# The chunk scan of a Mamba-2 SSD encoder in another order, its skip term as a TensorE product

## The reference, cut to what matters

```python
seg = acs[:, :, :, None] - acs[:, :, None, :]
decay_in = exp(where(tri, seg, NEG_INF))
cb = einsum('bctgn,bcsgn->bctsg', cc, bc)
y_diag = einsum('bctsg,bctsgh,bcsghp->bctghp', cb, decay_in, xdt)
states = einsum('bcsgn,bcsgh,bcsghp->bcghpn', bc, decay_out, xdt)
# scan over chunks: h = h * chunk_decay + states, prev = h before the chunk
y_off = einsum('bctgn,bcghpn,bctgh->bctghp', cc, prev, exp(acs))
# forward and backward direction, then
y = y_fwd + y_bwd + d_skip * xs
y = y * silu(z)                      # then a grouped RMSNorm
# gMLP: mixed = w_s @ v (per 128-token chunk) + b_s;  out = gelu(u) * mixed
```

## Time and profile before

| | |
|---|---|
| time before, median of 3 runs | 2483.04 us (2482.91 to 2487.15) |
| the profiled execution's own time | 2485.22 us |
| its span in the profile | 2483.4 us |
| TensorE matmul busy | 2426.9 us (98%) |
| VectorE, ScalarE, GpSimd busy | 1375.8, 998.4, 1263.1 us |
| granted TensorE clock, mean | 0.996 |
| scan, first state product to first y_turn, layer 0 | 65.25 us |
| the same in layer 1 | 65.85 us |

### The profile page before, as it was taken

How to read it: one execution, slowest core, us unless ns; L and a number is a source line. 1 busy time by engine, 2 the same in 40 slices (tenths; PEclk the granted TensorE clock), 3 DMA queues, 4 the chain that set the end, 5 groups by cost and what they waited for, 6 DMA issues and landing times.

```text
span 2483.4 us, 33046 instructions
## 1 busy us (share of the span) xinstructions
PE 2426.9 (98%) x12882; PEld 2072.2 (83%) x12882; DVE 1375.8 (55%) x1561; ACT 998.4 (40%) x1737; POOL 1263.1 (51%) x814
## 2 busy tenths in 40 slices
PE   7999999999999999999999999998999999999999
PEld 6989997887888888887898899977878888888887
DVE  4476557738655546428345765586385555544332
ACT  4345567613444344212024465585144344431110
POOL 3242113323977877666633311142349877866664
PEclk9999999999999999999999999999999999999999
DMA  4434444231222212654333334442212222226544
GB/s 160 136 114 125 134 139 149 81 119 68 85 79 91 85 68 85 217 178 132 130 121 94 110 128 151 134 136 90 89 64 102 85 70 100 83 90 201 174 141 142
DMA packets 102964, 290.68 MB, mean 117 GB/s; under 512 B 7800, under 2 KB 30328, under 8 KB 101112
## 3 DMA queue, kind: packets, MB, share of 16 engines
q1 hardware_dynamic: 80360, 255.73, 30.4%
q10 hardware_dynamic: 22456, 32.90, 4.1%
HBM read 229.84 MB, written 58.75 MB: 116 GB/s over the span
## 4 chain that ended last, share of the span: by engine, by line
PE 81%; DVE 9%; ACT 4%; POOL 3%; issue 2%; DMA 1%; SPq 0%; ACTq 0%; DVEq 0%; POOLq 0%
PE PS L690 20%; PE PS L694 20%; PE PS L693 20%; PE PS L775 3%; PE PS L779 3%; PE PS L778 3%; PE PS L945 2%; PE PS L934 2%; POOL WL L629 2%; DVE HL L1780 1%; PE PS L1116 1%; PE PS L1081 1%; PE PS L924 1%; PE PS L923 1%; ACT LG L1501 1%
## 5 line engine op out<-in xcount | busy, mean ns | idle before, releaser
L605 POOL CAST WH<-RAW 128x1024 fp32r<-128x1024 f32 x156 | 184.5, 1182 | 905.5 <-PE PS L690 327.1
L690 PE MATMUL PS<-HH,WH 128*128 128x512 f32 x1264 | 496.4, 393 | 3.6 <-ACT QS L1668 2.6
L694 PE MATMUL PS<-HH,WL 128*128 128x512 f32 x1264 | 493.3, 390 | 0.0
L693 PE MATMUL PS<-HL,WH 128*128 128x512 f32 x1104 | 430.5, 390 | 0.0
L607 POOL TENSOR_TENSOR WL<-RAW,WH 128x1024 fp32r<-128x1024 f32 x156 | 396.8, 2543 | 12.5
L690 PEld LDWEIGHTS PS<-HH,WH 128*128 128x128 f32 x1264 | 237.4, 188 | 56.5 <-DVE HL L1780 3.5
L694 PEld LDWEIGHTS PS<-HH,WL 128*128 128x128 f32 x1264 | 237.3, 188 | 51.9
L690 PE MATMUL PS<-AR,WH 128*128 128x512 f32 x704 | 276.0, 392 | 2.3 <-DVE X L2208 1.8
L694 PE MATMUL PS<-AR,WL 128*128 128x512 f32 x704 | 275.9, 392 | 0.0
L693 PE MATMUL PS<-AR,WH 128*128 128x512 f32 x704 | 275.2, 391 | 0.0
L775 PE MATMUL PS<-WH,HH 128*128 128x256 f32 (+1 forms) x896 | 261.0, 291 | 1.7 <-ACT KN L1307 1.3
(11 more groups left out here) (274 smaller groups left out, 4677.3 us busy)
## 6 DMA issues: line engine op xcount, KB each, us to landing
RAW<-wst SPq DMA_DIRECT2D x156, 512.0 KB, 3.5
TOE<-toe_d SPq DMA_DIRECT2D x64, 512.0 KB, 3.7
act_d<-CVV SPq DMA_DIRECT2D x22, 1024.0 KB, 4.0
ARL<-act_d SPq DMA_DIRECT2D x88, 256.0 KB, 3.3
RAW<-wst SPq DMA_DIRECT2D x20, 1024.0 KB, 4.9
RAWB<-wst SPq DMA_DIRECT2D x20, 1024.0 KB, 4.9
XBS<-xbc_d SPq DMA_DIRECT2D x24, 512.0 KB, 4.2
xbc_d<-CV ACTq DMA_DIRECT2D x16, 512.0 KB, 3.6
```

The source lines that it names most:

```text
L605: nc.gpsimd.tensor_copy(hi, raw).then_inc(hi_done, 1)
L690: ins = nc.tensor.matmul(out, wh, xh, start=first, stop=False, skip_group_check=onto)
L693: nc.tensor.matmul(out, wh, xl, start=False, stop=False, skip_group_check=onto)
L694: return nc.tensor.matmul(out, wl, xh, start=False, stop=last, skip_group_check=onto)
```

## The change

On TensorE the function `chunk` is cut into `outer`, `mixed` and `chunk` and put in another order. For chunk c it now issues: state product of c, sums 2 and 3 of c, four skip products of c, turn of c+1, sums 0 and 1 of c+1, outer products of c+1, gate mix of c+1, value product of c. The outer products and the gate mix of chunk 0 come ahead of the loop.

The skip term is now four float32 products of 128x128 by 128x128 on TensorE: x of the chunk (still channel by token, in `XBS`) against `DIAG`, a block of the diagonal with d_skip in it, into bank 4; the value products add to them. `DIAG` is made once a layer by one VectorE operation in `far`. GpSimd loses the multiplication L657 and one addition, and keeps one addition, Y1 + Y2, in chunks 1 to 6.

ScalarE makes `v_scaled` one chunk ahead, and that of chunk 0 ahead of the whole loop; `BC` becomes a double buffer and its wait is for an older `w_masked`. VectorE runs state sum and mask of c, then the outer parts and the gate of c+1, then the output of c.

```diff
+        DIAG = place("DIAG", [P, 4, P], u_at + 29952)
-        BC = work("BC", [P, 2, GROUPS, P])
+        BC = place("BC", [P, 2, 2, GROUPS, P], u_at + 25856)
...
# GpSimd
-                    pool.wait_ge(chunk_done, 1 + n)
-                    step.then(nc.gpsimd.tensor_tensor(by_head(Y3[:]), xs, per_head(par_("d_skip")), ALU.mult))
-                    if c < LINKS:
+                    if 0 < c < LINKS:
+                        pool.wait_ge(yz_ready, 2 + n)
+                        pool.wait_ge(y12_done, 1 + l * LINKS + c)
                         pool.wait_ge(y2_ready, l * LINKS + c + 1)
-                        ins = nc.gpsimd.tensor_tensor(Y3[:], Y3[:], Y2[:], ALU.add)
-                        if c:
-                            step.then(ins)
-                    if c:
-                        pool.wait_ge(y12_done, 1 + l * LINKS + c)
-                        ins = nc.gpsimd.tensor_tensor(Y3[:], Y3[:], Y1[:], ALU.add)
-                    ins.then_inc(y3_ready, 1)
+                        nc.gpsimd.tensor_tensor(Y3[:], Y1[:], Y2[:], ALU.add).then_inc(y3_ready, 1)
...
# TensorE, the new chunk
+                def chunk(c):
+                    n, par, end = l * NT + c, c % 2, c == NT - 1
+
                     if not end:
                         pe.wait_ge(bst_ready, n + 1)
                         pe.wait_ge(xw_ready, l * LINKS + c + 1)
                         pe.wait_ge(gt_done, n + 1)
...
                         last.then_inc(sf_full, 1)
+                    sums(n, 2)
+                    sums(n, 3)
+                    pe.wait_ge(chunk_done, 1 + n)
+                    for j in range(4):
+                        last = nc.tensor.matmul(PS[:, 4, j * P:(j + 1) * P], XBS[:, par, j, :], DIAG[:, j], start=(j == 0),
+                                                stop=False, skip_group_check=True)
+                    last.then_inc(xbs_used, 1)
+                    if not end:
+                        pe.wait_ge(xbs_full[1 - par], 16 * (l * 6 + 2 + c // 2 + par + 1))
+                        pe.wait_ge(bst_ready, n + 1)
+                        chunk_turn(c // 2, 1 - par)
                         sums(n + 1, 0)
                         sums(n + 1, 1)
+                        outer(c + 1)
+                        mixed(c + 1)
 
                     pe.wait_ge(xs_ready, n + 1)
-                    pe.wait_ge(chunk_done, 1 + n)
...
# ScalarE
+                v_scaled(0)
                 for c in range(NT):
...
-                    act.wait_ge(w_masked, 2 + n * 2)
-                    if c:
-                        act.wait_ge(sf_full, l * LINKS + c)
-                    A(BC[:].rearrange("p a g n -> p (a g n)"), bank(1), ACT.Copy).then_inc(bst_ready, 1)
+                    if n:
+                        act.wait_ge(w_masked, n * 2)
+                    if c >= 2:
+                        act.wait_ge(sf_full, l * LINKS + c - 1)
+                    A(BC[:, par].rearrange("p a g n -> p (a g n)"), bank(1), ACT.Copy).then_inc(bst_ready, 1)
...
-                        if j == 1:
-                            v_scaled(c)
+                        if j == 1 and c < LINKS:
+                            v_scaled(c + 1)
...
# VectorE, far() and the new loop
+                    TT(DIAG[:].rearrange("p j (a e) -> p j a e", a=2),
+                       ident.rearrange("p (a e) -> p a e", a=2).unsqueeze(1).to_broadcast((P, 4, 2, HD)),
+                       par_("d_skip").rearrange("p (j a) -> p j a", a=2).unsqueeze(3).to_broadcast((P, 4, 2, HD)), ALU.mult)
...
+                outer_parts(0)
+                for c in range(NT):
+                    if c < LINKS:
+                        state_sum(c)
+                    masked(c)
+                    if c < LINKS:
+                        outer_parts(c + 1)
+                    else:
+                        y_inverse(0, NT - 1)
+                        normalise(0)
+                        normalise(1)
+                    gated_out(c)
```

More of the change, by code:

```diff
@@ L1066, in sums, with outer @@
                                          skip_group_check=True).then_inc(ab_full, 1)
-                def chunk(i2, par, end):
-                    c = i2 * 2 + par
-                    n = l * NT + c
+                def outer(c):
+                    n, par = l * NT + c, c % 2
                     if c:
@@ L1074, in chunk @@
                         pe.wait_ge(y12_done, 1 + l * LINKS + c - 1)
-                    if not end:
+                    if c < LINKS:
                         pe.wait_ge(y2_ready, l * LINKS + c)
-                    for d in range(0 if c else 1, 1 if end else 2):
+                    for d in range(0 if c else 1, 2 if c < LINKS else 1):
                         for g in range(GROUPS):
@@ L1083, in chunk, with mixed @@
                     last.then_inc(yo_full, 1)
[L1084 to L1087 removed]
+                def mixed(c):
+                    pe.wait_ge(vn_ready, l * NT + c + 1)
                     for g in range(GG):
@@ L1127, in _ @@
                 pe.wait_ge(ra_done, 1 + (l + 1) * LINKS)
+                outer(0)
+                mixed(0)
                 for c in range(NT):
-                    chunk(c // 2, c % 2, c == NT - 1)
+                    chunk(c)
                 def y_turn(c):
@@ new lines, in by_head, with heads, outer_parts @@
+                def by_head(t):
+                    return t.rearrange("p (h e) -> p h e", h=HEADS)
+                def heads(t, c):
+                    return t[:, c, 0:8].unsqueeze(2).to_broadcast((P, HEADS, HD))
+                def outer_parts(c):
+                    n, par = l * NT + c, c % 2
+                    if c:
+                        dve.wait_ge(yo_full, n + 1)
+                        if c >= 2:
+                            dve.wait_ge(y3_ready, l * (LINKS - 1) + c - 1)
+                        TT(by_head(Y1[:]), by_head(bank(5)), heads(EACS, c), ALU.mult).then_inc(y12_done, 1)
+                    if 0 < c < LINKS:
+                        step.then(TT(by_head(CURF[:]), by_head(CURF[:]), heads(CDEC, c), ALU.mult))
+                    dve.wait_ge(mx_full, n + 1)
+                    dve.wait_ge(zg_full[par], 16 * (l * (NT // 2) + c // 2 + 1))
+                    TT(YT[:, c, INNER:INNER + GW], PS[:, 7, 0:GW], ZG[:, par, 2, :], ALU.mult).then_inc(gt_done, 1)
@@ new lines, in state_sum, with masked @@
+                def state_sum(c):
+                    dve.wait_ge(sf_full, l * LINKS + c + 1)
+                    if c:
+                        ins = TT(CURF[:], CURF[:], bank(7), ALU.add)
+                    else:
+                        ins = nc.vector.tensor_copy(CURF[:], bank(7))
+                    ins.then_inc(curf_ready, 1)
+                def masked(c):
+                    n, par = l * NT + c, c % 2
+                    dve.wait_ge(bst_ready, n + 1)
+                    for g in range(GROUPS):
+                        dve.wait_ge(exp_ready, 2 + n * 4 + 2 * g + 2)
+                        step.then(TT(SEG[par][:, 2 * g], SEG[par][:, 2 * g], SEG[par][:, 2 * g + 1], ALU.add))
+                        TT(SEG[par][:, 2 * g], SEG[par][:, 2 * g], BC[:, par, 1, g, :].unsqueeze(1).to_broadcast((P, 4, P)),
+                           ALU.mult).then_inc(w_masked, 1)
```

72 lines of the change are left out of this document (18 added, 54 removed).

## The result

The changed kernel takes **2506.94 us** (median of 4 runs, 2505.93 to 2508.08); the kernel before, on the same chip, 2484.72 (2482.91 to 2487.15). The ratio is 1.0083, with a 95% interval from 1.0071 to 1.0095: slower by 22.2 us, where 17 were forecast. The profiled execution took 2508.08 us, with a span of 2506.1.

A forecast was written before the change was run, and what follows sets the result against it. TensorE was taken as the bound, with a loop over Y2 in the new order: 2 x 6.7 + 2.1 + 1.4 = 16.9 us, the start 0, bringing 2483.04 to 2500.0 us; range 2489 to 2510.

The forecast's parts named there:

- the loop over Y2: Steady state: TensorE waits 0.67 us a chunk for ScalarE's Y2 before the outer products; period 9.91 us; chance 0.65.
- the rival of a second wait: Scan loop: XW or the gate comes late for the state product, +22 to +30 us, 2506 to 2511; chance 0.15.
- Skip products: Four added float32 products on TensorE: 0.90 us a chunk, 14.4 us in 16 chunks, hidden in the steady state.
- 0.05 for the signal: Last term of the Y2 chain: time from Y2's end to TensorE's outer products, 0.05 of 5.40 us.
- Six periods: First state product to that of chunk 6: 59.5 us against 52.76, +6.7 us a layer.
- The start: First state product of the scan at 408.8 against 408.79 before: 0, at best -0.7, at worst +1.3 us.
- The mask waits go: In the scans, TensorE's waits for VectorE's mask, 4.1 and 4.6 us, go, staying only in the last chunk.
- The end: From chunk 6's state product to the scan's end: 14.6 us with a clock loss, +2.1 and +1.4 by layer.
- Behind the scan TensorE is again the bound, so a later start stays: After the scan: the scan's lost time carries through; no further gain or loss was added to the 16.9 us.
- TensorE's work alone decides: Rival: Y2 comes in time, a chunk takes 9.24 us, +7.4 us in all (+5 to +8), 2490; chance 0.12.
- All waits vanish: Rival: with less GpSimd work, mask waits and the end's low clock go, 0 to +4 us, 2483; chance 0.08.

The follow-up runs named there:

- e8: The kernel before with the skip products on TensorE and GpSimd's one remaining addition made to wait for the chunk's masks: 2493.00 us.
- e7: The kernel before with GpSimd's addition of Y1 put first and its addition of Y2 waiting for the chunk's masks: 2479.11 us.
- e1: The changed kernel without the skip products and DIAG, the skip term left out of the result: 2504.22 us.
- e2: The changed kernel with ScalarE's Y2 moved ahead of the second set of the chunk's exponentials: 2500.61 us.
- e4: The changed kernel with the three GpSimd operations of before in place of the skip products: 2514.59 us.
- e5: The changed kernel with the skip term on GpSimd as before and ScalarE's Y2 moved ahead of the second exponentials: 2501.59 us.
- e9: e5 with GpSimd's two additions made to wait for the chunk's masks: 2513.31 us.
- e3: The kernel before, its chunk order kept, with DIAG and the skip products on TensorE and one addition left on GpSimd: 2514.92 us.
- e11: The kernel before with GpSimd's addition of Y2 waiting for the chunk's masks, the order of its two additions kept: 2486.46 us.

## Why the prediction was right, point by point

The direction and the mechanism in the steady state were right, and 2506.94 lies in the range of 2489 to 2510; the size was 5 us short (22.2 against 17; the stated 2500.0 is 6.9 short, as the kernel before measured 1.7 higher in this comparison). That it lies in the range is in part luck: the loop over Y2 alone had been given 2495 to 2505. What reached further up was the rival of a second wait, 2506 to 2511, and that wait didn't come; the misses came from other places. By its own steps:

- **Skip products, 0.90 us a chunk.** Measured 422.94 - 422.05 = 0.89. The estimate of 0.65 us, from the rate in the Trainium skill's page "TensorE: Matmul & The Clock Gate", section "Back-to-back issue gap", doesn't hold for this float32 form: the trace decides, and e8 against e7 shows 0.90 in each steady period. That they are hidden in the steady state is shown by e1.
- **The loop over Y2, 9.91 us.** The mechanism is shown by e1 and e2. The size was 10.08. Mis-sized was the term "0.05 for the signal": from the end of Y2 (423.80 + 1.80 = 425.60) to the outer products it is 0.15. It was taken from one row of the kernel before, a wait for one semaphore; the outer products wait for three, and all such waits took 0.15 (last section). The step from state product to the second record of sum 2 was 1.15, not 1.10, and the rest of the period 4.54, not 4.51. Together 0.17 a chunk, 2.0 us in twelve periods.
- **Six periods, +6.7 us a layer.** Measured +8.81 and +7.82. Beside the 1.0 of the longer period, the first period of layer 0 is 11.19, at a granted clock of 0.61 (below); in layer 1, at full clock, it is 10.09. The prediction had no clock term at the start.
- **The start, 0.** The first state product came at 409.02, against 408.79 before and 408.8 forecast: right. DIAG took 0.64 us where 0.67 was forecast. But the new start leaves TensorE idle ahead of it, and what follows from that wasn't in the sum.
- **The mask waits go, but for the last chunk.** Right: 1.0 us a layer.
- **The end, 14.6 us, +2.1 and +1.4.** The stretch to y_turn was 14.05 and 13.93, +1.56 and +0.75: the loss of clock that I added didn't fall there, and without it the 13.5 were 0.4 to 0.6 short. The step that failed is the sentence "Behind the scan TensorE is again the bound, so a later start stays". The stretch from y_turn to the output projection became 10.07 and 10.18 us, where it was 8.57: +1.50 and +1.61. Of this 0.62 and 0.74 lie ahead of the third turn (489.61 in layer 0). The turn of y is a hand-over between TensorE, VectorE and ScalarE, and VectorE came to it later: its last output starts 1.20 us behind y_turn (485.84 against 484.64), where it was 0.29 before (474.33 against 474.04). The other 0.87 in each layer lie behind the last turn, where the granted clock was 0.50 and 0.70 and before 1.00. The last turn of layer 0 to the output projection, before and changed:

```profile
480.31:482.61 2.30, 1.09 (x9) 0.89 (x9) 2.27 (x6) 1.39 (x3) 0.00 (x0) 1.00 0.00 0
491.54:494.71 3.17, 1.97 (x9) 1.59 (x9) 2.99 (x8) 1.35 (x3) 0.00 (x0) 0.50 0.00 0
```

So a loss of clock near the 0.9 to 1.4 of the prediction did come in each layer, but in a stretch to which it gave nothing. In e1 neither part is there: its last output starts 0.43 us behind y_turn, the granted clock behind the last turn is 1.00, and the whole stretch is 8.57.
- **The sum.** 0.23 + 8.81 + 7.82 + 1.56 + 0.75 + 1.50 + 1.61 = 22.3 us of the 22.7 by which the span grew. The 0.4 left are spread over the rest of the program. Forecast were 16.9: 2.1 of the difference come from the six periods of layer 0, 1.1 from those of layer 1, 1.9 from both ends taken together with the turn of y, and 0.2 from the start. Of the 2.1, 1.1 are the longer first period at the low clock.
- **The rivals.** "TensorE's work alone decides" is what the kernel does once Y2 is early (e2, period 9.23, though the first periods and the end kept it at 2500.6 instead of 2490). "A second wait in the loop" didn't come: the one wait of TensorE for the gate, 0.7 us a layer, is at the first state product. (Its heading says +22 to +30 us; its own sum of 2506 to 2511 is +23 to +28.) A gate that is late because GpSimd holds up VectorE does come in e4, e5 and e9, where the skip term is on GpSimd. "All waits vanish" fell to the loop, as forecast, but its mechanism was the more important one. That a GpSimd operation and a VectorE operation with two SBUF inputs exclude each other, by the Trainium skill's page "SBUF — State Buffer", section "SBUF: two separate sides", is borne out by e3 (masks of 1.78 and 1.42 us instead of 0.69), e7 and e8 (0.69 again where GpSimd waits). The prediction used it for the waits that the new order would remove; e7 has them removed in the old order, and that is the gain that the change was not needed for.

## What to carry to other kernels

When work is moved ahead to fill a gap, look at what the moved work waits for, and follow that chain once around the loop: here it started at the very product that it was put behind. An operation of GpSimd is judged by what it falls beside more than by its length: with fewer of them e3 was 22 us slower than e8, where the same ones wait for the mask (15 of the 22 lie in the periods without a low clock), and e7, with all of them and one moved behind the mask, is 7 us faster than the kernel before. Such a wait pays only where there is slack behind it (e9 and e11 had none).

## What the runs showed of the hardware

- **A VectorE operation with two SBUF inputs and a GpSimd operation beside each other: the one that began second pays.** In e3 the mask operation began 0.11 us behind GpSimd's addition (444.11 and 444.00) and took 1.78, where 0.69 is usual; 0.56 of it lie behind the addition's end (445.33). The next began 0.62 behind XW and took 1.42, 0.55 of it behind XW's end. Where VectorE began first, GpSimd paid: in e4 L666 took 1.59 us, where 1.27 is usual, behind VectorE's mask of 482.47. An operation of VectorE with an input in PSUM paid nothing: in e5 the state addition CURF<-CURF,PS began at 450.81 beside GpSimd's multiplication (450.75 to 451.79) and took 0.69.
- **From the end of an operation to the product that waited for it took 0.05 us or 0.15, whichever engine it came from.** In the changed kernel it was 0.15 from ScalarE's Y2 to the outer products (425.60 to 425.75), but 0.05 from ScalarE's scaling of ST to the gate mix of chunk 0 (407.04 to 407.09). From VectorE's masks of the last chunk it was 0.15 to the first group of the value product (482.20 to 482.35) and 0.05 to the second (483.53 to 483.58). In the scans of eleven of the kernels here the short time stands where the program waits for one semaphore ahead of the product (second group, decay sums, gate mix), the long one where it waits for two or three (first group, CURF outer products, state product). No run varied this, so it is not shown to be the cause.

```profile
481.51 0.69 DVE L2174 TENSOR_TENSOR SEG<-SEG,BC 128x512 f32<-128x512 f32 x1
482.84 0.69 DVE L2174 TENSOR_TENSOR SEG<-SEG,BC 128x512 f32<-128x512 f32 x1
```

- **The clock fell behind an emptier stretch.** In the changed kernel TensorE was busy 5.81 of the 9.00 us ahead of the first state product of layer 0, and the granted clock was 0.61 in the 4.38 us behind it, near the 1.2 GHz level; the first state product took 1.79 us instead of 1.08, and the first period 11.19. In the kernel before the same two stretches were:

```profile
399.79:408.79 9.00, 7.68 (x46) 5.94 (x45) 7.67 (x13) 7.03 (x24) 2.84 (x2) 1.00 0.62 222
408.79:413.40 4.61, 3.91 (x27) 3.50 (x26) 3.97 (x5) 3.02 (x12) 2.81 (x2) 1.00 0.10 40
```

It doesn't follow each time: in layer 1 of the changed kernel TensorE was busy 5.78 of the 9.00 us ahead of the first state product, the granted clock behind it was 1.00, and the first period was 10.09. Over all kernels here: of the 14 first state products in the new order, with TensorE busy 5.8 to 6.4 of the 9.00 us ahead, six were followed by a granted clock of 0.61, never both of one run; of the 12 in the old order, with 7.4 to 7.7, none. What decides between the layers stays open; no run tried it.
